# Forgetting attention's value products once a head, with the values stationary on two column halves, and its gate with features on partitions

## The chip, the core and the metric

The kernel runs on one core of a Trainium2 chip. A core has TensorE (the 128x128 array; PE is its matmul queue and PEld its weight loads in the profile), VectorE (DVE), ScalarE (ACT), GpSimd (POOL) and SyncE (SP), which issues most transfers. Each engine works through its own instructions in order and waits on semaphores for the others. The metric is device time in microseconds (us), the median of the runs; lower is better.

## The reference, cut to what matters

Three transformer blocks follow each other on 512 tokens of width 1024. The change touches only the first block, whose input projection is cut into three mixers. The third is forgetting attention, with 8 heads of 64 features:

```python
def _fox_mixer(q, k, v, f_logit, b_f):
    qh, kh, vh = heads(q), heads(k), heads(v)
    log_f = jax.nn.log_sigmoid(f_logit + b_f)
    c = jnp.cumsum(jnp.transpose(log_f, (0, 2, 1)), axis=-1)
    for blk in range(seq // C_BLOCK):          # 4 blocks of 128 queries
        q0, q1 = blk * C_BLOCK, blk * C_BLOCK + C_BLOCK
        s = einsum('bhqd,bhkd->bhqk', qh[:, :, q0:q1], kh[:, :, :q1]) * scale
        s = s + c[:, :, q0:q1, None] - c[:, :, None, :q1]
        p = softmax(where(mask, s, -inf), axis=-1)
        outs.append(einsum('bhqk,bhkd->bhqd', p, vh[:, :, :q1]))
...
y_c = _fox_mixer(c_q, c_k, c_v, c_fl, fox_b_f[layer]) * jax.nn.silu(c_z)
y = jnp.concatenate([y_a, y_b, y_c], axis=-1)
x = x + jnp.einsum('bse,ed->bsd', y, w_out[layer])
```

Query block t looks at the first 128(t+1) keys only, so a head has 1 + 2 + 3 + 4 = 10 pairs of a query tile and a key tile.

## The kernel before, in words

**Dense products.** Every projection is a `Block` of 512 (or 256) columns. The contraction runs over eight chunks of 128 features in four units of two chunks. Activations and weights are each split into a high and a low part (`hH`, `hL`, `wH`, `wL`), and three products replace one. A block of orientation "tok" puts tokens on the output's partitions (activations stationary), one of orientation "feat" puts features there (weights stationary). ACT makes `wH` of the next unit and DVE makes `wL` (`split`), from `wraw`, which SP loads three units ahead.

**The softmax loop.** Attention runs in steps s, one item (head h, query tile t) a step, head by head: items 4h to 4h+3 are head h. Each engine has its own loop, and in step s:

- PE makes the scores of item s in one of two banks (four matmuls, the last two add the decay row and the causal mask), then one side group (six matmuls of a dense block), then transposes the weights of item s-2, then, before the change, the value products of item s-3. The side groups are those of `UV` (512 columns) in steps 0 to 15 and of `AZ` (256 columns) in steps 16 to 35; in steps 1, 5, 9, ..., 29 there is none (`FOX_IDLE`).
- DVE, before the change, first finishes item s-4 (reciprocal of the row sum, then the product with the gate, from PSUM into `merged`), then takes the row maximum of item s, then does extra work of the other two mixers (`gated_mlp`) and splits.
- ACT takes the exponential of item s, copies the transposed weights of item s-2 out of PSUM, then does splits and its part of the extras.
- POOL subtracts for the low part of each head's keys (L602).

**By feature.** Two other attentions of the program, grouped-query (`gqa`) and neighbourhood (`nat`), already work in another form. DVE scales the exponentials of item s-1 by the reciprocal row sum before they are transposed. Once a head, in a step with s % 4 == 2, `head_values` multiplies with the values stationary (64 columns of the array) and the weights moving, the even key tiles on one column half and the odd on the other. In the next step ACT copies one half out of PSUM (L1297) and DVE adds the other (L1955). The result has features on partitions and needs no transposes.

**After the loop.** The block's output product `O0` needs the merged rows with features on partitions. PE transposes chunks 4 to 7 (forgetting attention) and 2 and 3 (the second mixer), ACT and DVE make `hH` and `hL` of each, and `O0` takes its units in the order 4, 6, 2, 0. Chunks 0 and 1 (the gMLP) come in the middle of `O0`.

## Time and profile before

| | before |
|---|---|
| median of 3 runs | 2502.22 us (2500.92 to 2503.83) |
| profiled execution | 2504.66 us, of which the span is 2502.9 us |
| PE busy | 2468.2 us, 99% |
| DVE busy | 1497.7 us, 60% |
| ACT busy | 1111.4 us, 44% |
| POOL busy | 68.8 us, 3% |
| granted TensorE clock, mean | 0.996 |

Times in the trace count from the span's start. The softmax loop of forgetting attention lies at 190.6 to 274.3 us, 3% of the span. PE's busy time includes modelled ends of pipelined matmuls, so the share says little by itself; what counts is how far apart successive instructions start and what an engine waited for.

### The profile page before, as it was taken

To read this page: it belongs to the slowest core of one execution; us is meant where nothing else is said; L and a number is where in the kernel's file an instruction comes from. 1 tells how busy PE (TensorE), PEld (TensorE's weight loads), DVE (VectorE), ACT (ScalarE), POOL (GpSimd) and SP (SyncE) were. 2 spreads that over 40 slices of the span, in tenths; PEclk is the share of its full clock that TensorE was granted. 3 is DMA by queue.
4 is the path that set the end of the run, shared out by engine and by line. 5 is a ranking of instruction groups with operands and counts; after the bars stand their busy time and mean duration, and the time that the engine had idled before them with its cause. 6 is when DMAs were issued, how large, how long until landed. Compare 5 with 4: busy or idle time off the path is not lost.

```text
span 2502.9 us, 31797 instructions
## 1 busy us (share of the span) xinstructions
PE 2468.2 (99%) x12090; PEld 2008.3 (80%) x12090; DVE 1497.7 (60%) x2798; ACT 1111.4 (44%) x1959; POOL 68.8 (3%) x148
## 2 busy tenths in 40 slices
PE   8999999999999999999999999999999999999998
PEld 7888878788777787888888887887787888888887
DVE  6766768653656677544444587645557686544445
ACT  3436455333645656322222344336647572422223
POOL 0001000100000000000000000000000000000000
PEclk9999999999999999999999999999999999999999
DMA  4320223223323231233333242233232212333332
GB/s 151 91 69 22 78 84 124 59 88 93 97 72 94 87 91 51 73 113 101 93 101 93 77 139 66 75 96 110 64 97 80 88 58 89 101 97 97 97 97 88
DMA packets 118967, 221.69 MB, mean 89 GB/s; under 512 B 14352, under 2 KB 21824, under 8 KB 118304
## 3 DMA queue, kind: packets, MB, share of 16 engines
q1 hardware_dynamic: 114192, 201.60, 26.7%
q0 software_dynamic: 4480, 17.79, 2.4%
q8 instruction: 97, 1.59, 0.3%
q14 instruction: 54, 0.44, 0.1%
q10 hardware_dynamic: 144, 0.26, 0.0%
HBM read 215.40 MB, written 4.23 MB: 88 GB/s over the span
## 4 chain that ended last, share of the span: by engine, by line
PE 92%; DVE 4%; ACT 3%; issue 1%; DMA 0%; SPq 0%; ACTq 0%; DVEq 0%
PE bank L686 51%; PE bank L683 28%; PE bank L833 2%; PE bank L910 1%; PE bank L809 1%; PE bank L844 1%; PE bank L810 1%; PE bank L859 1%; PE bank L894 1%; PE bank L948 1%; PE bank L727 0%; DVE tab L1876 0%; ACT sbufPT L1293 0%; ACT sbufS L1279 0%; DMA wraw<-in_w_in_dram 0%
## 5 line engine op out<-in xcount | busy, mean ns | idle before, releaser
L1682 DVE TENSOR_TENSOR wL<-wraw,wH 128x1024 fp32r<-128x1024 f32 (+1 forms) x388 | 460.7, 1187 | 661.0 <-ACT wH L1115 659.1
L1115 ACT ACTIVATE wH<-wraw 128x1024 fp32r<-128x1024 f32 (+1 forms) x388 | 398.5, 1027 | 932.8 <-PE bank L686 576.4
L686 PE MATMUL bank<-hH,wH 128*128 128x512 f32 x1704 | 684.6, 402 | 1.9 <-DVE wL L1682 1.0
L686 PE MATMUL bank<-hL,wH 128*128 128x512 f32 x1704 | 666.0, 391 | 0.0
L686 PE MATMUL bank<-hH,wL 128*128 128x512 f32 x1704 | 665.6, 391 | 0.0
L686 PEld LDWEIGHTS bank<-hH,wH 128*128 128x128 f32 x1704 | 320.6, 188 | 76.0 <-issue 10.5
L686 PEld LDWEIGHTS bank<-hL,wH 128*128 128x128 f32 x1704 | 320.7, 188 | 71.4 <-issue 7.7
L686 PEld LDWEIGHTS bank<-hH,wL 128*128 128x128 f32 x1704 | 320.4, 188 | 68.5
L683 PE MATMUL bank<-wH,hH 128*128 128x512 f32 (+2 forms) x736 | 283.4, 385 | 0.0
L683 PE MATMUL bank<-wL,hH 128*128 128x512 f32 (+2 forms) x736 | 278.3, 378 | 0.0
L683 PE MATMUL bank<-wH,hL 128*128 128x512 f32 (+2 forms) x736 | 278.1, 378 | 0.0
L683 PEld LDWEIGHTS bank<-wH,hH 128*128 128x128 f32 x736 | 139.5, 190 | 26.0 <-DVE wL L1682 0.5
L683 PEld LDWEIGHTS bank<-wL,hH 128*128 128x128 f32 x736 | 139.0, 189 | 25.8
L683 PEld LDWEIGHTS bank<-wH,hL 128*128 128x128 f32 x736 | 139.3, 189 | 24.0
L683 PE MATMUL bank<-wH,yH 128*128 128x512 f32 x352 | 137.2, 390 | 0.0
L683 PE MATMUL bank<-wH,yL 128*128 128x512 f32 x352 | 137.0, 389 | 0.0
L683 PE MATMUL bank<-wL,yH 128*128 128x512 f32 x352 | 136.9, 389 | 0.0
L833 PEld LDWEIGHTS bank<-ident,sbufS 128*128 128x128 f32 x592 | 70.2, 140 | 45.6 <-issue 21.0
L833 PE MATMUL bank<-ident,sbufS 128*128 128x128 f32 x592 | 98.4, 276 | 5.9 <-ACT sbufPT L1293 5.1
L686 PE MATMUL bank<-yH,wH 128*128 128x512 f32 x256 | 100.4, 392 | 0.9 <-ACT yH L1189 0.5
L686 PE MATMUL bank<-yL,wH 128*128 128x512 f32 x256 | 100.0, 391 | 0.2
L686 PE MATMUL bank<-yH,wL 128*128 128x512 f32 x256 | 99.7, 389 | 0.0
(346 smaller groups left out, 3062.8 us busy)
## 6 DMA issues: line engine op xcount, KB each, us to landing
wraw<-in_w_in_dram SPq DMA_DIRECT2D x180, 512.0 KB, 3.6
wraw<-in_w_ffn_down_dram SPq DMA_DIRECT2D x44, 512.0 KB, 3.5
wraw<-in_w_ffn_gate_dram SPq DMA_DIRECT2D x40, 512.0 KB, 3.7
wraw<-in_w_ffn_up_dram SPq DMA_DIRECT2D x40, 512.0 KB, 3.7
wraw<-in_w_out_dram SPq DMA_DIRECT2D x24, 512.0 KB, 3.5
wraw<-in_w_up_a_dram SPq DMA_DIRECT2D x8, 512.0 KB, 3.5
wraw<-in_w_up_b_dram SPq DMA_DIRECT2D x8, 512.0 KB, 3.5
wraw<-in_w_up_c_dram SPq DMA_DIRECT2D x8, 512.0 KB, 3.5
```

The lines of the kernel that those rows point to most:

```text
L683: mm = pe.matmul(bank[t][:, 0:b.cols], act_part[:, k, t * P:(t + 1) * P], w_part[:, kk, :], start=first, stop=last)
L686: mm = pe.matmul(bank[b.bank0 + t][:, :], w_part[:, kk, t * P:(t + 1) * P], act_part[:, k, :], start=first, stop=last)
L809: pe.matmul(dst[:, 0:kmax], q_split[slot][:, tok], k_twice[slot][:, keys], start=True, stop=False)
L810: mm = pe.matmul(dst[:, 0:kmax], q_split[slot][:, tok], k_low[slot][:, keys], start=False, stop=kind != "fox")
L833: mm = pe.transpose(bank[TP][:, c * P:(c + 1) * P], sbufS[:, y % 3, c * P:(c + 1) * P], ident[:, :])
L844: mm = pe.matmul(bank[PV][:, 0:w], sbufPT[:, y % 2, c * P:(c + 1) * P], v[:, c, c0:c0 + w], start=c == 0, stop=c == nk - 1)
L859: mm = pe.matmul(bank[PV][half, :].rearrange("p (t q) -> p t q", t=NT), v[:, c, c0:c0 + w], weights[:, :, c * P:(c + 1) * P], start=c < 2, ...
L894: pe.matmul(bank[SC + pair % 2][:, :], k1[:, h, j * P:(j + 1) * P], q1[:, h, :], start=True, stop=True).then_inc(S["qk_done"], 1)
L910: mm = pe.matmul(dst[:, 0:P + 1], pmat[:, back, sj, t * P:(t + 1) * P], v1a[:, sj, h, :], start=sj == srcs[0], stop=sj == srcs[-1])
L948: mm = pe.matmul(bank[SC + h][:, tok], kl[r, h // 2, tok], ql[r, h // 2, tok], start=True, stop=True)
L1115: A(wH[:, u % W_SLOTS, 0:width], wraw[:, u % RAW_SLOTS, 0:width], ACT.Copy).then_inc(S["w_hi"], 1)
L1682: V.tensor_tensor(wL[:, u % W_SLOTS, 0:width], wraw[:, u % RAW_SLOTS, 0:width], wH[:, u % W_SLOTS, 0:width].bitcast(F32), ALU.subtract).th ...
```

## The change

- `CZ`, the gate's projection, goes from "tok" to "feat", so that the gate lies in `merged` with features on partitions. It has as many matmuls of the same size as before.
- Forgetting attention joins the by-feature form. DVE scales the exponentials before the transposes, `head_values` makes one head's products in four matmuls of 512, 384, 128 and 256 moving columns, ACT copies 384 columns of the other half, and DVE adds the halves and multiplies by the gate. The transposed weights of a head go to `tab` (free by then) instead of `sbufPT`.
- ACT never writes the first 128 tokens of a head's half (key tile 1 isn't seen from query tile 0), so POOL zeroes `ytok[:, :, 0:128]` once.
- The 16 transposes of chunks 4 to 7 fall away. ACT and DVE make `hH` and `hL` of them straight from `merged`, after chunks 2 and 3, and `O0` takes its units in the order 2, 4, 6, 0.
- POOL's load of `final_norm_g` into `ytok` waits for the last head.

```diff
-        "CZ": Block("CZ", w, 0, KD, 3328, 512, "tok"),
-        "O0": Block("O0", o, 0, KD, 0, 512, "tok", order=(4, 6, 2, 0)),
+        "CZ": Block("CZ", w, 0, KD, 3328, 512, "feat"),
+        "O0": Block("O0", o, 0, KD, 0, 512, "tok", order=(2, 4, 6, 0)),
...
 def by_feature(kind):
-    return kind in ("gqa", "nat")
+    return kind in ("fox", "gqa", "nat")
...
+            pool.wait_ge(S["ho_done"], 4)
+            pool.wait_ge(S["low_zero"], 1)
+            pool.memset(ytok[:, :, 0:P], 0.0).then_inc(S["y_zero"], 1)
+            pool.wait_ge(S["y_zero"], 1)
...
-            pool.wait_ge(S["y_ready"], 1)
+            pool.wait_ge(S["y_done"], 32)
             pool.dma_start(yflat[:, 0:D], bcast_rows(a["final_norm_g"], D)).then_inc(S["gp_step"], 16)
...
                 pe.wait_ge(S["ptev"], y + 1)
-                pe.wait_ge(S["y_done"], y + 1 - NT)
-                if kind == "gqa":
+                if y >= NT:
+                    pe.wait_ge(S["y_done"], y + 1 - NT)
+                if kind == "fox":
+                    own, other, _ = feature_rows(it)
+                    for c, half in ((0, own), (1, other), (3, own), (2, other)):
+                        mm = pe.matmul(bank[PV][half, c * P:SEQ].rearrange("p (t q) -> p t q", t=NT - c),
+                                       v[:, c, c0:c0 + w], weights[:, c:NT, c * P:(c + 1) * P], start=c < 2, stop=c >= 2)
+                elif kind == "gqa":
...
-            pe.wait_ge(S["y_done"], n.at("ys"))
-            transposes(merged, (4, 5, 6, 7), None, 0)
             transposes(merged, (2, 3), "y_ready", 1)
+            n("tp", 4)
+            n("tp_hi", 4)
...
                         own, other, g = feature_rows(items[s - 4])
+                        tokens = slice(P if kind == "fox" else 0, SEQ)
                         act.wait_ge(S["pv_done"], nth_y[s - 4] + 1)
-                        A(ytok[own, g, :], bank[PV][other, :], ACT.Copy).then_inc(S["half_moved"], 1)
+                        A(ytok[own, g, tokens], bank[PV][other, tokens], ACT.Copy).then_inc(S["half_moved"], 1)
...
-            hi_chunks((4, 5, 6, 7), hH, lambda k: 0.5)
             hi_chunks((2, 3), hH, lambda k: 0.5)
+            act.wait_ge(S["y_done"], n.at("ys"))
+            for j in range(4):
+                n("tp")
+                A(hH[:, 4 + j, :], merged[:, j, SEQ:D], ACT.Copy, scale=0.5).then_inc(S["tp_hi"], 1)
...
                         then(V.reciprocal(r, total))
-                        if kind == "fox":
-                            dst = merged[:, it["t"], SEQ + it["y"]:SEQ + it["y"] + w]
-                            V.scalar_tensor_tensor(out=dst, in0=src, scalar=r, in1=dst, op0=ALU.mult,
-                                                   op1=ALU.mult).then_inc(S["y_done"], 1)
-                        else:
-                            dst = ytok[:, it["t"], it["y"]:it["y"] + w]
-                            V.tensor_scalar(dst, src, r, None, ALU.mult).then_inc(S["y_done"], 1)
+                        dst = ytok[:, it["t"], it["y"]:it["y"] + w]
+                        V.tensor_scalar(dst, src, r, None, ALU.mult).then_inc(S["y_done"], 1)
...
                         dve.wait_ge(S["half_moved"], n("half_moved"))
-                        V.tensor_tensor(ytok[own, g, :], ytok[own, g, :], bank[PV][own, :], ALU.add).then_inc(
-                            S["y_done"], NT)
+                        if kind == "fox":
+                            if s == 7:
+                                dve.wait_ge(S["y_zero"], 1)
+                            then(V.tensor_tensor(ytok[own, g, :], ytok[own, g, :], bank[PV][own, :], ALU.add))
+                            z = merged[own, g, SEQ:D]
+                            V.tensor_tensor(z, z, ytok[own, g, :], ALU.mult).then_inc(S["y_done"], NT)
+                        else:
+                            V.tensor_tensor(ytok[own, g, :], ytok[own, g, :], bank[PV][own, :], ALU.add).then_inc(
+                                S["y_done"], NT)
...
-            lo_chunks((4, 5, 6, 7), hH, hL, lambda k: 0.5)
             lo_chunks((2, 3), hH, hL, lambda k: 0.5)
+            for j in range(4):
+                n("tp")
+                dve.wait_ge(S["tp_hi"], n("tp_hi"))
+                V.scalar_tensor_tensor(out=hL[:, 4 + j, :], in0=merged[:, j, SEQ:D], scalar=0.5,
+                                       in1=hH[:, 4 + j, :].bitcast(F32), op0=ALU.mult, op1=ALU.subtract).then_inc(
+                    S["tp_free"], 1)
```

Three places show how instructions move; line numbers after the change are a few higher than before. The first is VectorE in steps 19 and 20. L1929 is the row maximum, L1896 and L1899 finish an older item, L1838 to L2232 are extras. Before:

```order
L1896 RECIPROCAL small<-small 128x1
L1899 SCALAR_TENSOR_TENSOR merged<-bank,small,merged 128x64
L1929 TENSOR_REDUCE small<-bank 128x1
L1838 TENSOR_REDUCE small<-set 128x16
L1896 RECIPROCAL small<-small 128x1
L1899 SCALAR_TENSOR_TENSOR merged<-bank,small,merged 128x64
L1929 TENSOR_REDUCE small<-bank 128x1
L2231 TENSOR_SCALAR small<-small 128x16
```

After, where L1939 is the row maximum, L1945 and L1946 scale the exponentials, L1968 adds the halves and L1970 multiplies by the gate:

```order
L1939 TENSOR_REDUCE small<-bank 128x1
L1945 RECIPROCAL small<-small 128x1
L1946 TENSOR_SCALAR sbufS<-sbufS,small 128x384
L1968 TENSOR_TENSOR ytok<-ytok,bank 64x512
L1970 TENSOR_TENSOR merged<-merged,ytok 64x512
L1853 TENSOR_REDUCE small<-set 128x16
L1939 TENSOR_REDUCE small<-bank 128x1
L1945 RECIPROCAL small<-small 128x1
L1946 TENSOR_SCALAR sbufS<-sbufS,small 128x512
L2248 TENSOR_SCALAR small<-small 128x16
```

The finishing product of 64 columns, which stood ahead of the maximum, is replaced by a scaling as wide as the item behind it, and in the step with s % 4 == 3 the sum and the gate's product stand between the scaling and the next maximum, behind a wait for ACT's copy.

The second place is PE in step 14, from the side group's last matmuls to the next item's scores. Before:

```order
L683 MATMUL bank<-wH,hH 128x512
L683 MATMUL bank<-wH,hL 128x512
L683 MATMUL bank<-wL,hH 128x512
L833 MATMUL bank<-ident,sbufS 128x128
L844 MATMUL bank<-set,sbufPT 128x64 x4
L809 MATMUL bank<-yL 128x512
```

After:

```order
L687 MATMUL bank<-wH,hH 128x512
L687 MATMUL bank<-wH,hL 128x512
L687 MATMUL bank<-wL,hH 128x512
L864 MATMUL bank<-tab,set 64x512
L864 MATMUL bank<-tab,set 64x384
L864 MATMUL bank<-tab,set 64x128
L864 MATMUL bank<-tab,set 64x256
L837 MATMUL bank<-ident,sbufS 128x128
L813 MATMUL bank<-yL 128x512
```

The value products of every step (L844, here those of one item) become four matmuls a head ahead of the transpose, in every fourth step.

The third place is PE at the end of the loop, from the last side group to the first matmuls of `O0`, as the difference; 24 transposes become 8.

```order
-L683 MATMUL bank<-wH,hH 128x256
-L683 MATMUL bank<-wH,hL 128x256
-L683 MATMUL bank<-wL,hH 128x256
-L727 MATMUL bank<-ident,merged 128x128 x24
-L683 MATMUL bank<-wH,hH 128x512
+L687 MATMUL bank<-wH,hH 128x256
+L687 MATMUL bank<-wH,hL 128x256
+L687 MATMUL bank<-wL,hH 128x256
+L731 MATMUL bank<-ident,merged 128x128 x8
+L687 MATMUL bank<-wH,hH 128x512
```

## Rows read from the trace of the kernel before

**Rows 1.** The page: busy time of each engine.

```profile
PE 2468.2 (99%) x12090; PEld 2008.3 (80%) x12090; DVE 1497.7 (60%) x2798; ACT 1111.4 (44%) x1959; POOL 68.8 (3%) x148
```

**Rows 2.** Stretches: head 2, the later heads by DVE's steps, two units of `O0`.

```profile
core 0: us, PE busy (x) PEld busy (x) DVE busy (x) ACT busy (x) POOL busy (x), PEclk, DMA share, GB/s
...
211.35:221.15 9.80, 9.80 (x67) 8.38 (x66) 4.68 (x14) 5.93 (x15) 1.78 (x1) 1.00 0.11 28
...
221.86:268.00 46.14, 43.80 (x322) 38.07 (x320) 39.56 (x95) 35.46 (x88) 6.19 (x4) 1.00 0.13 41
...
277.38:282.90 5.52, 5.52 (x27) 4.56 (x26) 3.12 (x5) 1.86 (x3) 0.00 (x0) 1.00 0.23 72
```

**Rows 3.** Who DVE waited for, 221.86 to 268.00 (us, times, longest).

```profile
DVE set L2202 <- ACT set L1395: 1.6, 1, 1.6
DVE small L1896 <- PE bank L844: 1.1, 3, 0.7
DVE set L2214 <- ACT set L1410: 1.0, 2, 0.5
DVE small L1929 <- PE bank L815: 0.8, 3, 0.4
DVE wL L1682 <- ACT wH L1115: 0.5, 1, 0.5
DVE yL L1852 <- ACT yL L1228: 0.2, 1, 0.2
```

**Rows 4.** PE in order of time, steps 22 and 23: start, length, what.

```profile
247.36 0.97 PEld L844 LDWEIGHTS bank<-set,sbufPT 128*128 128x128 f32 x8
...
248.28 0.48 PE L809 MATMUL bank<-yL 128*128 128x512 f32 x1
...
249.12 0.37 PE L683 MATMUL bank<-wH,hH 128*128 128x256 f32 x1
```

**Rows 5.** The same view, grouped-query attention: one head's values.

```profile
649.06 1.94 PE L859 MATMUL bank<-tab,set 128*64 128x512 f32 x8
```

**Rows 6.** DVE in order of time, steps 19 and 20.

```profile
240.83 0.68 DVE L1929 TENSOR_REDUCE small<-bank 128x1 f32<-128x512 f32 x1
...
242.68 0.16 DVE L1896 RECIPROCAL small<-small 128x1 f32<-128x1 f32 x1
242.87 0.28 DVE L1899 SCALAR_TENSOR_TENSOR merged<-bank,small,merged 128x64 f32<-128x64 f32 x1
243.07 0.28 DVE L1929 TENSOR_REDUCE small<-bank 128x1 f32<-128x128 f32 x1
```

**Rows 7.** Lines of DVE: scaling (two widths), sum, product of two tensors (ns min/median/max).

```profile
L1936 DVE TENSOR_SCALAR sbufS<-sbufS,small x32: 485/487/491, 626.5 to 713.1; 128x512 f32<-128x512 f32 x32
...
L1936 DVE TENSOR_SCALAR sbufS<-sbufS,small x32: 352/354/355, 781.9 to 851.8; 128x256 f32<-128x256 f32 x32
...
L1955 DVE TENSOR_TENSOR ytok<-ytok,bank x32: 678/686/693, 643.9 to 1939.7; 64x512 f32<-64x512 f32 x32
...
L1719 DVE TENSOR_TENSOR x<-x,ytok x4: 691/692/692, 305.3 to 309.3; 128x512 f32<-128x512 f32 x4
```

**Rows 8.** ACT in order of time behind the maximum at 240.83.

```profile
241.55 0.69 ACT L1281 ACTIVATE sbufS<-bank,small 128x512 f32<-128x512 f32 x1 [2.11 <-DVE small L1929]
...
242.23 0.38 ACT L1293 ACTIVATE sbufPT<-bank 128x256 f32<-128x256 f32 x1
```

**Rows 9.** Waits in grouped-query (first) and neighbourhood attention (second).

```profile
DVE ytok L1955 <- ACT ytok L1297: 10.1, 6, 1.8
...
PEld bank L833 <- DVE sbufS L1936: 4.0, 8, 0.9
```

**Rows 10.** The end of the loop and start of `O0`, in order of time.

```profile
268.00 0.15 DVE L1896 RECIPROCAL small<-small 128x1 f32<-128x1 f32 x1
...
274.86 0.42 DVE L1821 SCALAR_TENSOR_TENSOR merged<-set,bank 128x256 f32<-128x256 f32 x1 [0.26 <-ACT set L1155]
...
277.41 0.49 PE L683 MATMUL bank<-wH,hH 128*128 128x512 f32 x1
```

More of the change, by code:

```diff
@@ L458, in head_weights @@
         def head_weights(kind):
-            return view(tflat, 0, (NT, SEQ)) if kind == "gqa" else view(ptflat, 0, (NT, NAT_KEYS))
+            return view(ptflat, 0, (NT, NAT_KEYS)) if kind == "nat" else view(tflat, 0, (NT, SEQ))
         gained = view(gflat, 0, (NT, SEQ))
@@ L480, in build @@
             vn_ready mix_done lam_dot lam_exp out_done a_ready y_squared low_zero
-            scan_out scan_rows m_done p_scaled half_moved
+            scan_out scan_rows m_done p_scaled half_moved y_zero
         """.split()
@@ L1286, in softmax @@
                         if by_feature(kind):
-                            act.wait_ge(S["pv_done"], y - it["t"])
-                            turned = head_weights(kind)[:, it["t"], :]
+                            if y >= NT:
+                                act.wait_ge(S["pv_done"], y - it["t"])
+                            turned = head_weights(kind)[:, it["t"], 0:it["kmax"]]
                         else:
```

## The prediction

> **What bounds the kernel now.** The page's busy times come first [rows 1]: PE is busy 99% of the span, DVE 60%. That suggests that any PE time saved is time won. But the change lies in 84 us, so I read the stretches there next [rows 2]. In head 2 (head 1 reads the same) PE is busy all 9.80 us and DVE 4.68: PE bounds. From DVE's step 12 (its maximum of item 12, at 221.86) to its step 32 (268.00) it is another picture: of 46.14 us DVE is busy 39.56. Third, DVE's waits there [rows 3]: they add up to 5.2 us, 1.9 on PE and 3.3 on ACT. The remaining 1.4 us are gaps between instructions. So DVE has 5.2 us to spare in 46, and that is what the reader should carry into the change, which gives PE less work and DVE more.
>
> **PE's side of the change.** A step's four value products are eight records, whose weight loads start 0.11 us apart ((0.97 - 0.19) / 7) [rows 4]. Ten pairs a head are 20 records, 2.2 us. Afterwards a head has four matmuls of 512, 384, 128 and 256 columns, 1280 in all. Grouped-query attention has four of 512 in 1.94 us, also on two halves [rows 5]; by columns that is 1.2 us, and I take 1.25. A saving of 1.0 us a head, 8 in all, if PE is what everything waits for. `CZ` keeps its number and size of matmuls, so nothing there.
>
> The Trainium skill (TensorEngine Tiling (Array Packing), Stationary-Streaming Swap in Performance Considerations) recommends just this swap where the moving side is 64 wide or less. By the row a head costs 1.25 us; if the halves did not overlap it would be about 2.1, and PE's saving would be gone.
>
> **DVE's side, head by head.** Removed: four finishing products, which start 0.20 us ahead of what follows [rows 6] though they last 0.28; 0.8 us. The reciprocals stay (0.19 to what follows). Added:
> - Four scalings. 512 columns take 0.487 and 256 take 0.354 [rows 7]; by the slope 384 take 0.42 and 128 take 0.29. Less the same 0.08 of overlap each: 1.22 us.
> - The sum of the halves, 0.69, and as its successor waits for it, 0.72 [rows 7].
> - The gate's product, two tensors of 512 columns: 0.69 by the nearest row [rows 7], 0.61 with overlap. Its bounds are 0.4 (two scalings' rate) and 0.7.
>
> That is 1.22 + 0.72 + 0.61 - 0.8 = 1.75 us more a head. Steps 12 to 31 hold five such heads: 8.7 us.
>
> **The new wait.** In the step with s % 4 == 3 DVE takes the maximum of item s, scales item s-1, and then waits for ACT's copy of the other half. ACT, in order, first has to take the exponential of item s (which needs that very maximum), then copy the transposes of s-2. From the row at 240.83: ACT begins at +0.72, its copy of 256 columns at +1.40 [rows 6, 8], the half's copy 0.31 later and takes 0.49 (an estimate from 0.38 for 256 columns), so DVE's sum starts at +2.25. DVE is through with its scaling at 0.60 + 0.19 + 0.42 = 1.21. It stands still for 1.04 us, however far PE is ahead, and nothing of its own lies between. Five heads: 5.2 us. Grouped-query attention shows the same wait: 10.1 us in 6 times [rows 9], 1.7 each, with PE's part in it. Behind the waiting sum stand on DVE the gate's product, the extras, the weight split and the next maximum; ACT's next exponential and PE's transposes two steps on wait for these.
>
> **The middle, summed.** DVE's work is 39.56 + 1.4 + 8.7 = 49.7 us, already over the 46.14 it had. With 5.2 of the new wait it is 54.9; I let all 5.2 of the old waits vanish, since DVE now arrives late everywhere. PE has 43.80 - 5 = 39 us of work there, so DVE bounds and PE stands. The middle grows by 8.7 us. Bounds: the gate's product at 0.4 takes 1.0 off; ACT's part of the old waits staying adds 3.3.
>
> **Before it.** By step 12 PE has saved 21 pairs (4.7 us) less two heads of 1.25: 2.2 us. But DVE is late once. After PE's step 7 ends, ACT still needs 0.2 + 0.31 + 0.49 and DVE 0.72 + 0.61 = 2.3 us till the next maximum, and in that step a weight split of 1.2 stands in between. The scaling of item 7 (0.20 + 0.19 + 0.49 later) is then ready at +4.4. PE gets to its transpose after 2.6 us: scores, about 0.4 and 0.5 (0.84 for 512 columns, [rows 4]), six side matmuls of 0.23 (24 in 5.52 us, [rows 2]), three transposes of 0.11. It waits 1.8. So PE's step 12 begins 0.4 earlier, at 220.7, but DVE's maximum in it comes 2.3 behind that instead of 0.7: at 223.0 or so, 1.2 late.
>
> **Behind it.** From DVE's step 32 to the first matmul of `O0` it was 9.4 us [rows 10]. Afterwards DVE has: a scaling with reciprocal 0.6, two extras of 1.2, a split of 1.2, four gates of the gMLP at 0.36, the sum and product 1.3, then two low chunks 1.3: 8.3 us, without a gap that I see. 1.0 us is won. The 16 dropped transposes don't count for more: ACT and DVE make chunks 2 and 3 while PE has nothing else. The four other chunks (0.62 on ACT and 0.68 on DVE each) lie under the first unit of `O0`, 5.5 us. POOL's memset waits for the second mixer's last output, before step 0, and what stands behind it in POOL's queue, the low keys of head 2, is asked for in step 4 at the earliest. Its load of the gain moves from step 31 behind the last head and is used after `O0`, some 22 us later; both cost nothing. Without that cover the load would add its few us once. SP's queue has the same transfers in the same order, but for the units of `O0`.
>
> **Sum.** 8.7 + 1.2 - 1.0 = 8.9 us. The profiled execution, 2504.66, becomes 2513.6; it stands 2.4 above the median, so the median of 2502.2 becomes 2511.
>
> **A page's rule on the product.** A head's gate product costs 0.61 us by a row of equal form. The Trainium skill (VectorE: DVE Perf Modes, Mode 2x_2P) says that a float32 tensor_scalar out of SBUF runs twice as fast as a float32 tensor_tensor. The trace agrees: 256 more columns cost the scaling 0.133 us [rows 7], and 512 of two tensors 0.69. By the other rate the sum would be 1.6 us less over eight heads.
>
> **The rivals.**
> - *Forecast: DVE bounds from step 12 on, and its wait for ACT is new.* 0.5. 2508 to 2514.
> - *The wait is covered.* DVE's extra work counts, but the half's copy is there in time. Neighbourhood attention speaks for it, where PE waited for the scaling only 4.0 us in 8 times [rows 9]; against it, there table work lies in the gap and here nothing does. 8.9 - 5.2 gives 2506; with the cheaper product 2505. 0.2.
> - *PE bounds throughout; the other side.* DVE follows PE all the way. Then 8 x 1.0 and 1.0 at the end are won: 2493 to 2495. It decides if DVE's additions a head stay under its spare 1.0 us (5.2 / 5) in the middle; they are 1.75 without any wait. 0.06. Something between this and no change, 0.06.
> - *The old waits stay or more come.* ACT's extras and splits go on being late (3.3 us), or the halves don't overlap (0.9 a head in heads 1 and 2), or PE's idle time brings its clock down, which is 1.00 through the loop [rows 2]: 2514 to 2519. 0.18.
> - The Trainium skill (TensorEngine Tiling, PSUM Bottleneck) warns that tiling speeds TensorE but not the emptying of PSUM, which may become the limit. Here it would be the forecast's way, since the half's copy and sum are that emptying.
>
> **How the numbers follow.** About 0.2%, 5 us, is what a measurement of this kernel can tell from none. The forecast and the last rival lie over +5 us: 0.68, of which I move 0.02 to no change for times at 2507. Within it: the covered wait (0.2), that 0.02 and half of the middle case (0.03), 0.25. Faster: 0.09, the other side and the rest. The range takes the covered wait in below from 2504 and most of the added waits above, to 2517; about 0.1 is left out on either side.
>
> **What would show it.** In the trace of the changed kernel: DVE's stretch from its maximum of item 12 to the reciprocal of item 31 should be near 55 us, with waits of about 1 us in front of the sum (L1968) on ACT's copy in all late heads; PE should wait for the scaling (L1946) before transposes (L837), some 8 to 12 us in all. The four value products should take 1.2 to 1.3 us. `O0` should start near 286. I am wrong if DVE shows idle time on PE of more than 3 us in that stretch, or if the sum waits for nothing.

## The result, and the profile after

| | before | after |
|---|---|---|
| median | 2502.34 us (2500.92 to 2503.83, 4 runs) | 2522.93 us (2521.97 to 2528.45, 4 runs) |
| profiled execution / its span | 2504.66 / 2502.9 | 2521.97 / 2520.2 |
| PE busy | [rows 1] | 2460.5 us, 98% |
| DVE busy | [rows 1] | 1512.3 us, 60% |
| granted clock, mean | 0.996 | 0.995 |

The ratio is 1.0085 (95% interval 1.0071 to 1.0100): slower by 20.6 us. The forecast was 2511 (2504 to 2517). The direction was right, the size less than half of what came.

The page after, busy times (line numbers after the change: scores L813 to L819, transposes L837, value products L864, maximum L1939, scaling L1946, sum L1968, gate product L1970, ACT's copy of the transposes L1304 and of the half L1309):

```profile
PE 2460.5 (98%) x11978; PEld 1995.4 (79%) x11978; DVE 1512.3 (60%) x2814; ACT 1115.4 (44%) x1967; POOL 68.0 (3%) x149
```

PE lost 7.7 us of work and DVE gained 14.6, and the median rose by 20.6 (the two profiled executions differ by 17.3). PE, which was busy 99% of the span, has less to do than before, so what was lost is waiting. The stretches that answer to [rows 2] (length, then busy times of PE, PEld, DVE, ACT, POOL, the granted clock, the DMA share, GB/s):

```profile
220.53:285.04 64.51, 43.64 (x260) 34.26 (x258) 50.31 (x105) 39.62 (x94) 5.32 (x4) 0.89 0.10 29
285.04:294.01 8.97, 5.95 (x32) 4.69 (x32) 8.17 (x15) 4.82 (x11) 0.56 (x1) 0.81 0.23 66
```

From the maximum of item 12 to the reciprocal of item 31 it was 46.14 us and is 64.51, 18.4 more where 8.7 were forecast. The way to `O0` takes 8.97. The mean clock of that stretch is 0.89; it was 1.00. DVE's waits in it, and those of PE's weight loads (us in total, times, longest):

```profile
DVE ytok L1968 <- ACT ytok L1309: 6.9, 5, 2.5
DVE small L1939 <- PE bank L819: 4.4, 4, 2.7
DVE set L2219 <- ACT set L1407: 1.0, 1, 1.0
...
PEld bank L837 <- DVE sbufS L1946: 17.2, 6, 4.0
```

DVE waits 12.3 us, not 5.2: for the half as foretold, but also 4.4 us for scores. An engine that is the bound doesn't wait for the one behind it. And PE stands 17.2 us for the scaling, up to 4.0 at a time. One head in order of time (start, length, what, idle time before and its releaser) shows both:

```profile
242.04 0.68 DVE L1939 TENSOR_REDUCE small<-bank 128x1 f32<-128x512 f32 x1
...
244.34 0.69 DVE L1968 TENSOR_TENSOR ytok<-ytok,bank 64x512 f32<-64x512 f32 x1 [1.10 <-ACT ytok L1309]
245.14 0.69 DVE L1970 TENSOR_TENSOR merged<-merged,ytok 64x512 f32<-64x512 f32 x1
245.86 1.22 DVE L1853 TENSOR_REDUCE small<-set 128x16 f32<-128x1024 f32 x1
247.11 0.29 DVE L1939 TENSOR_REDUCE small<-bank 128x1 f32<-128x128 f32 x1
...
247.51 0.49 DVE L1946 TENSOR_SCALAR sbufS<-sbufS,small 128x512 f32<-128x512 f32 x1
247.79 0.48 ACT L1304 ACTIVATE tab<-bank 128x384 f32<-128x384 f32 x1
248.42 1.08 PE L837 MATMUL bank<-ident,sbufS 128*128 128x128 f32 x4 [3.52 <-ACT tab L1304]
...
254.28 0.69 DVE L1939 TENSOR_REDUCE small<-bank 128x1 f32<-128x512 f32 x1 [0.87 <-PE bank L819]
```

A head falls into two parts, and these carry all that follows. The **near part** runs from the maximum of the head's widest item (item 19, 512 columns, at 242.04) to that of the next head's first (item 20, 247.11). The **far part** runs from there to the next widest item (254.28). In the near part DVE has, one behind the other, the wait for the half, the sum, the product and an extra of 1.22 us, and only then the maximum of item 20 and the scaling of item 19, for which PE stands since 244.9. The same two parts of four heads each, first of the kernel before (items 15 to 28), then of the changed one; the first row is one near part, the second row the sum of the four near ones, the third that of the far ones:

```profile
240.83:243.07 2.24, 1.92 (x15) 1.74 (x15) 2.17 (x5) 1.05 (x3) 0.00 (x0) 1.00 0.64 202
...
sum 9.19, PE 8.45 PEld 7.71 DVE 8.91 ACT 6.08 POOL 0.03; mean PE 2.11 PEld 1.93 DVE 2.23 ACT 1.52 POOL 0.01
...
sum 26.91, PE 25.39 PEld 21.93 DVE 21.83 ACT 21.33 POOL 4.89; mean PE 6.35 PEld 5.48 DVE 5.46 ACT 5.33 POOL 1.22
```

```profile
242.04:247.11 5.07, 1.64 (x13) 1.27 (x12) 3.77 (x7) 1.53 (x4) 0.00 (x0) 1.00 0.36 107
...
sum 21.76, PE 9.92 PEld 8.49 DVE 15.20 ACT 9.54 POOL 0.00; mean PE 2.48 PEld 2.12 DVE 3.80 ACT 2.38 POOL 0.00
...
sum 30.22, PE 24.62 PEld 18.94 DVE 24.10 ACT 20.43 POOL 4.03; mean PE 6.16 PEld 4.73 DVE 6.03 ACT 5.11 POOL 1.01
```

Before, DVE was busy 97% of the near parts and PE 94% of the far ones. Of DVE's 5.4 us of idle time here 5.1 lay in the far parts. The change adds 6.3 us of DVE's work and 5.8 us of waits for the half to the near parts, which grow from 9.19 to 21.76. The far parts grow from 26.91 to 30.22, though PE has less to do there.

### The profile page after: what moved, and what is told of

It reads as the page before. It is cut to its first block, busy times and chain, and to the rows that moved or that the text cites. A ratio compares the mean times of both kernels' runs of the same rounds, so it can differ in the third digit from the quotient of the medians.

```text
span 2520.2 us, 31577 instructions
## 1 busy us (share of the span) xinstructions
PE 2460.5 (98%) x11978; PEld 1995.4 (79%) x11978; DVE 1512.3 (60%) x2814; ACT 1115.4 (44%) x1967; POOL 68.0 (3%) x149
## 4 chain that ended last, share of the span: by engine, by line
PE 90%; DVE 5%; ACT 3%; issue 2%; DMA 0%; SPq 0%; ACTq 0%; DVEq 0%
PE bank L690 51%; PE bank L687 26%; PE bank L837 2%; PE bank L920 1%; PE bank L813 1%; PE bank L814 1%; PE bank L869 1%; PE bank L904 1%; PE bank L848 1%; PE bank L958 1%; DVE hL L1800 1%; DVE tab L1891 0%; PE bank L731 0%; DVE sbufS L1936 0%; DMA wraw<-in_w_in_dram 0%
## 5 line engine op out<-in xcount | busy, mean ns | idle before, releaser
L690 PE MATMUL bank<-hH,wH 128*128 128x512 f32 x1736 | 696.9, 401 | 1.6 <-ACT hH L1199 0.9
L690 PE MATMUL bank<-hL,wH 128*128 128x512 f32 x1736 | 678.1, 391 | 0.0
L690 PE MATMUL bank<-hH,wL 128*128 128x512 f32 x1736 | 677.5, 390 | 0.0
L690 PEld LDWEIGHTS bank<-hH,wH 128*128 128x128 f32 x1736 | 326.4, 188 | 77.7 <-issue 11.1
L690 PEld LDWEIGHTS bank<-hL,wH 128*128 128x128 f32 x1736 | 326.3, 188 | 72.4 <-issue 7.7
L690 PEld LDWEIGHTS bank<-hH,wL 128*128 128x128 f32 x1736 | 326.2, 188 | 69.8
L687 PE MATMUL bank<-wH,hH 128*128 128x512 f32 (+2 forms) x704 | 270.8, 385 | 2.3 <-DVE hL L1800 2.3
L687 PE MATMUL bank<-wH,hL 128*128 128x512 f32 (+2 forms) x704 | 265.7, 377 | 0.0
L687 PE MATMUL bank<-wL,hH 128*128 128x512 f32 (+2 forms) x704 | 265.7, 377 | 0.0
L687 PEld LDWEIGHTS bank<-wH,hH 128*128 128x128 f32 x704 | 133.9, 190 | 26.9 <-DVE hL L1800 2.5
L837 PE MATMUL bank<-ident,sbufS 128*128 128x128 f32 x592 | 100.9, 281 | 27.8 <-ACT tab L1304 21.1
L837 PEld LDWEIGHTS bank<-ident,sbufS 128*128 128x128 f32 x592 | 71.2, 142 | 70.0 <-DVE sbufS L1946 30.1
```

What stands on the lines that cost most here:

```text
L687: mm = pe.matmul(bank[t][:, 0:b.cols], act_part[:, k, t * P:(t + 1) * P], w_part[:, kk, :], start=first, stop=last)
L690: mm = pe.matmul(bank[b.bank0 + t][:, :], w_part[:, kk, t * P:(t + 1) * P], act_part[:, k, :], start=first, stop=last)
L837: mm = pe.transpose(bank[TP][:, c * P:(c + 1) * P], sbufS[:, y % 3, c * P:(c + 1) * P], ident[:, :])
```

## The experiments

I kept four theories. A: DVE's load sets the pace. B: the halved clock behind PE's waits is part of the loss. D, later sharpened to E: what counts is where DVE's work stands, ahead of what PE waits for. F: ACT's copies, in order behind exponentials that wait for DVE, carry its lateness on. "Near" and "far" in this table are the four parts of items 15 to 31 together in the profiled execution, in us, worked out from the starts of DVE's maxima. Each ratio is to the kernel before in the same rounds, whose median was 2501.5 to 2502.4 us. Where the intervals of two rows overlap, their medians alone don't tell them apart.

| kernel | median us | ratio to before (95%) | near | far |
|---|---|---|---|---|
| before | 2502.3 | | 9.19 | 26.91 |
| after | 2522.9 | 1.0085 (1.0071 to 1.0100) | 21.76 | 30.22 |
| after, again | 2524.7 | 1.0092 (1.0077 to 1.0107) | 21.77 | 30.32 |
| fillers, first try | 2538.3 | 1.0141 (1.0126 to 1.0156) | 21.83 | 40.32 |
| fillers in the value bank, from step 17 | 2521.7 | 1.0076 (1.0061 to 1.0091) | 21.80 | 26.46 |
| the same, from step 9 | 2521.6 | 1.0082 (1.0067 to 1.0097) | 21.78 | 26.97 |
| load alone, near | 2514.0 | 1.0045 (1.0030 to 1.0060) | 14.94 | 30.62 |
| load alone, far | 2506.6 | 1.0020 (1.0010 to 1.0029) | 9.34 | 29.86 |
| scaling alone | 2506.4 | 1.0016 (1.0006 to 1.0025) | 10.24 | 28.47 |
| sum and product later | 2512.3 | 1.0040 (1.0025 to 1.0055) | 9.84 | 33.01 |
| the same, copy first | 2508.8 | 1.0028 (1.0018 to 1.0038) | 9.83 | 30.64 |
| one half | 2510.8 | 1.0034 (1.0022 to 1.0046) | 12.74 | 29.60 |
| one half, extras later | 2509.2 | 1.0031 (1.0020 to 1.0042) | 8.40 | 33.70 |
| the same, copy first | 2506.1 | 1.0014 (1.0005 to 1.0024) | 8.29 | 30.70 |
| one half, all later | 2514.1 | 1.0051 (1.0036 to 1.0066) | 6.45 | 40.23 |
| the same, copy first | 2508.6 | 1.0020 (1.0010 to 1.0030) | 6.12 | 34.19 |
| after without scaling | 2528.2 | 1.0102 (1.0085 to 1.0119) | 22.16 | 32.63 |
| the same, copy first | 2521.1 | 1.0074 (1.0057 to 1.0091) | 22.11 | 28.85 |
| after, copy first | 2523.0 | 1.0083 (1.0068 to 1.0098) | 21.86 | 29.10 |
| before, copy first | 2502.0 | 0.9997 (0.9988 to 1.0006) | 9.59 | 26.45 |

**Sum and product one step later** (the changed kernel):

```
-  if by_feature(kind) and s >= 7 and s % NT == 3:
-      own, _, g = feature_rows(items[s - 4])
+  late = int(kind == "fox")
+  if by_feature(kind) and s >= 7 + late and s % NT == (3 + late) % NT:
+      own, _, g = feature_rows(items[s - 4 - late])
```

> The changed kernel, with one edit: DVE's sum of the two halves and the gate's product stand one step later for forgetting attention, behind the next maximum and the next scaling, so that ACT's copy of the other half has been there for long. Theory A (DVE's work and its wait for ACT's half copy are what sets the loop's pace): the five waits of 1.1 to 2.5 us in front of the sum (6.9 us in steps 12 to 31) go, PE's wait for the next scaling gets shorter by about as much, and the time falls by 5 to 8 us, to 2515 to 2518. Theory B (the larger part of the loss is PE's halved clock after its long waits): the waits for the scaling fall under 3 us, the clock stays at 1.00 through the loop, and the time falls by more than the waits removed: 10 us or more, under 2513. Rival C (ACT's own work or PE is what the loop waits for, and DVE's wait only fills slack): no change, 2521 to 2525.

2512.3, 10.6 less, with the same work. That is more than the waits removed (6.9). The trace still shows the clock at half from 246 to 250 us and a DVE wait of 2.71 for PE behind it. Which theory owns the surplus this run doesn't tell; the fillers below put the clock at some 3 us, which would cover it but doesn't prove it.

**All value products on the head's own half** (four matmuls into `bank[PV][own]`, no half copy, no sum):

> The changed kernel with the value products of forgetting attention all on the head's own column half: no copy of the other half by ACT, no sum by DVE, and no zeroing by POOL; DVE multiplies the gate with the bank directly. A head costs PE about 0.9 us more, DVE 0.7 less, ACT 0.4 less, and the wait of about 1.1 us is gone. Theory A: 1.8 us a head less on DVE over six heads is 11 less, and 1 to 2 more where PE bounds in the first heads: 2511 to 2514. Theory B: as PE's waits get shorter the clock stays up as well: 2505 to 2509. Rival C (the emptying of the bank is no bound, PE's matmul time counts): 2524 to 2530.

2510.8, just under A's range and above B's, at a clock of 1.00 from item 12 to the end of the loop.

**The scaling alone, in the kernel before** (`by_feature` scaling and PE's wait for it in fox too; the finishing product no longer scales):

> The kernel before with one edit: DVE scales the exponentials of forgetting attention by the reciprocal ahead of the transposes, as in the changed kernel, and the value products stay per item as before, with a finishing product that no longer scales. This adds 1.22 us a head to DVE (four scalings less overlap) and puts DVE between the exponential and PE's transposes; PE's work is that of before. Theory A: DVE has 5.2 us to spare in steps 12 to 31 and gets 6.1 more: 2503 to 2506. Theory B: PE's dependence on the scaling brings waits of several us and a lower clock by itself: 2508 to 2516. Rival C: the scaling costs nothing: 2501 to 2503.

2506.4: 4.0 more, just above A's range and well below B's. DVE's eight times 1.22 us are paid to two fifths. So putting DVE between the exponential and the transposes costs little by itself.

**Fillers, first try** (ten matmuls of 512 columns behind ACT's last copy, before the wait for the scaling):

> The changed kernel with ten matmuls more of 512 columns (their result is never read) on PE in steps 17, 21, 25, 29 and 33 of forgetting attention, between the scores and the transposes that wait for the scaling: they fill about 2.2 us of the 4 us that PE stands there. They are put there to keep its clock from falling. Theory B (the four stretches at half clock, 17 us together, make PE late for DVE): the granted clock stays at 1.00 up to the end of the loop, and the time falls by 4 to 8 us, to 2515 to 2519. Theory A alone (DVE paces the loop, PE at half clock has time enough): the clock stays up and the time is the same within 1 us, 2522 to 2524. If the fillers end later than the scaling, the time rises by up to 5 us.

2538.3, outside all that was expected. The fillers' row shows why:

```profile
256.88 4.64 PE L831 MATMUL bank<-hH 128*128 128x512 f32 x10 [3.44 <-ACT tab L1308]
```

PE had already stood 3.44 us for the copy. The clock had fallen, each filler took 0.46 us, and they ended behind the scaling. It only shows what late work on PE costs there.

**Fillers in the bank of the value products:**

```
   elif by_feature(kind):
+      if kind == "fox" and s in (17, 21, 25, 29, 33):
+          pe.wait_ge(S["y_done"], nth_y[s - 2] + 1 - NT)
+          for _ in range(8):
+              pe.matmul(bank[PV][:, :], hH[:, 0, 0:P], hH[:, 1, :], start=True, stop=True)
       pe.wait_ge(S["p_scaled"], n("p_scaled"))
```

> The filler once more, where it can start early. In the run with ten fillers PE first stood 3.4 us until ACT had copied the transposes before, the clock fell, and the fillers ran at half of it and ended after the scaling, so that run said nothing on the clock. Here eight matmuls of 512 columns go into the bank of the value products, which is free once DVE has made the last head's gate product, about 1 us after PE's scores; 1.7 us at full clock, in steps 17, 21, 25, 29 and 33. Theory B (the halved clock behind the waits is what makes the loop longer than the forecast): PE's waits without work are under 2 us, the granted clock is 1.00 up to the last head, and the time falls by 3 to 7 us against the changed kernel, to 2516 to 2520. Theory A alone (DVE's work and its wait are all of the loss): the clock stays up and the time is 2522 to 2524.

2521.7. The clock is 1.00 from 218 us to the end of the loop, and the time barely moves: it misses B's 2516 to 2520 and lies beside A's 2522 to 2524.

**The same in steps 9 and 13 too, beside the changed kernel again:**

> The changed kernel once more, unchanged, so that the fillers and the other edits have it beside them on the same chip. All theories: 2522 to 2524, with a spread of some us from the heads in which the clock happens to fall.

> The fillers of the bank of the value products (eight matmuls of 512 columns) in steps 9 and 13 too, so that no head from the second on is left with a wait of 3 us and more; in the run before the clock had fallen at 212 to 218 us, ahead of the first filler, and stayed at 1.00 behind it. Theory B (part of the loss is the halved clock): the clock is 1.00 from 196 us to the end of the loop, and the time is 3 to 5 us under that of the changed kernel in the same rounds. Theory A alone: within 1 us of it.

2521.6 against 2524.7 in the same rounds, 3.1 less; the intervals overlap. (The changed kernel itself came 0.7 above the 2522 to 2524 expected.) The profiled stretches say it more sharply. The far parts with fillers:

```profile
235.73:244.15 8.42, 6.32 (x44) 4.72 (x43) 7.23 (x19) 6.18 (x15) 1.28 (x1) 1.00 0.00 0
249.23:255.87 6.64, 6.64 (x34) 4.98 (x33) 5.50 (x12) 5.86 (x14) 1.39 (x1) 0.78 0.00 0
260.19:266.39 6.20, 5.98 (x38) 4.40 (x37) 5.99 (x14) 5.37 (x13) 1.38 (x1) 1.00 0.27 89
273.35:279.06 5.71, 4.89 (x33) 3.35 (x32) 5.38 (x13) 2.85 (x9) 0.00 (x0) 1.00 0.28 92
sum 26.97, PE 23.83 PEld 17.45 DVE 24.10 ACT 20.25 POOL 4.05; mean PE 5.96 PEld 4.36 DVE 6.03 ACT 5.06 POOL 1.01
```

The clock was still at half for a moment in the second, so the expectation of 1.00 throughout did not hold. But the sum is 26.97, that of before, and the near parts keep their 21.78. So B is right for some 3 us: the growth of the far parts is the halved clock. In these four heads the whole rest of the loss stands in the near parts, 3.15 us a head. In the changed kernel the near parts of heads 1 and 2 grew too, from 2.30 to 5.11 and from 2.24 to 4.02.

**Load without dependency, near and far** (the kernel before, two unread products a head; the first in s % 4 == 3, the second in s % 4 == 1):

```
+  if kind == "fox" and s >= 7 and s % NT == 3:
+      g = 2 + (s // NT) % 2
+      then(V.tensor_tensor(ytok[0:DH, g, :], q2[0:DH, 0, :], q2[0:DH, 1, :], ALU.mult))
+      then(V.tensor_tensor(ytok[0:DH, g, :], q2[0:DH, 0, :], q2[0:DH, 1, :], ALU.mult))
   if extra:
```

> The kernel before, with DVE's load alone: in each step with s % 4 == 3 from 7 on DVE makes two tensor products more of 64 by 512 (two of 0.7 us, 1.4 a head; their result is never read), where the changed kernel has its sum and gate product. Nothing waits for them but what stands behind them on DVE. Theory A: 1.4 by five heads is 7 us in a stretch where DVE had 5.2 us of waits: these go first, so +2 to +4 us at the loop's end: 2504 to 2506. Theory D (load without a dependency is hidden; the loss comes from the path): 2502 to 2503.

> The kernel before with the same eight pairs of unread tensor products (1.4 us a head) as in the run with the load alone, but in the steps with s % 4 == 1 instead of 3, ahead of the extras. In s % 4 == 3 they cost 11.9 us, 8 x 1.4 = 11.2. Theory A (any us of DVE's counts when DVE has used up its waits): again 8 to 12 us, 2510 to 2514. Theory E (only what stands between the maximum of a head's widest item and the maximum of the next head's first item is on the chain through DVE, ACT and PE; elsewhere PE's work lies beside it): 2 to 6 us, 2504 to 2508.

11.9 us near and 5.1 far, for the same eight pairs. That is the cleanest evidence for E. The eight places don't match at the ends: two near pairs (steps 31 and 35) stand behind the last maximum and one far pair (step 33), and from item 3 to item 15 neither place costs more than 0.3 us. But in the four heads of items 15 to 31, where both kernels have four pairs, it is 9.5 us against 3.1. Near, the near parts grow by 5.75 (the load's full length), and the far parts by 3.7, with the clock at half for 3.4 us in three of the four. Far, the heads' far parts grow by 0.82, nothing, 0.76 and 1.37:

```profile
242.68:250.57 7.89, 7.42 (x43) 6.50 (x44) 4.52 (x13) 6.08 (x14) 1.29 (x1) 0.78 0.01 2
```

```profile
240.56:246.98 6.42, 6.15 (x46) 5.17 (x45) 6.15 (x15) 5.86 (x14) 1.28 (x1) 1.00 0.04 14
```

The first row is the far part behind a loaded near part: the clock is 0.78 and it takes 7.89. The second holds the load itself, DVE 6.15 instead of 5.27, and takes the 6.42 of before.

**The scaling left out of the changed kernel** (DVE's `tensor_scalar` skipped, PE waits for the exponential):

> The changed kernel without the scaling of the exponentials: DVE still takes the reciprocals, but forgetting attention's weights are not divided by their sum (that part of the computation is left out), and PE's transposes wait for ACT's exponential alone. The wait for ACT's half copy, the sum and the gate's product stay. This takes 1.22 us a head off DVE and takes DVE out of the path from the exponential to the transposes. Theory A (DVE's load counts, each us of it): 5 to 6 heads of 1.22 are 6 to 7 us less, 2515 to 2517. Theory D (the scaling's place in the path, behind DVE's sum, product and extras, is what makes PE stand, and its clock fall): PE's waits of 3 to 4 us go, the clock stays at 1.00, and the time falls by 12 us or more, under 2511.

2528.2, the wrong way for both. PE stood at the same place as long, for another releaser:

```profile
PEld bank L839 <- ACT sbufS L1293: 16.4, 5, 4.1
...
PE bank L839 <- ACT tab L1306: 15.8, 5, 4.0
```

In the head shown above, ACT's copy of item 18 (247.79) stands behind the exponential of item 20, which waits for the same maximum. This began F. (The expectations below call these items 14 and 16; by the count in the trace they are 18 and 20.)

**Extras later, all later** (one-half kernel; first the extra of s % 4 == 3 goes behind the widest item's scaling, then the product too):

> The kernel with all value products on one half, with one edit more: in the steps with s % 4 == 3 DVE's extra work (a grouped sum or a product of up to 1.22 us) stands behind the next maximum and the scaling of the head's widest item instead of ahead of them. DVE's work is the same. Theory A (DVE's load alone): no change against that kernel, 2509 to 2512. Theory D (what stands ahead of the scaling that PE waits for is what costs): PE's waits for the scaling get up to 1.2 us shorter in four heads, DVE's waits for the next scores (4.5 us) get shorter behind them, 2505 to 2508.

> The kernel with the values on one half, where DVE's gate product stands one step later and the extras of s % 4 == 3 behind the scaling of the widest item: between the maximum of the widest item and the maximum of the next head's first item DVE has one scaling and at most a weight split. DVE's work is that of the one-half kernel (45.9 us in steps 12 to 31 and 1.5 of gaps). Theory E: DVE's other waits shrink to 1 or 2 us, and the time is 2 to 5 us under the run with the extras alone moved (2509.2): 2504 to 2507. Theory A (load alone): 2508 to 2510. Rival: ACT's exponential of the next item is not what PE waits for, and the later product only delays the bank: over 2510.

2509.2 is A's number, not D's: DVE still waited 4.3 us for scores. The near parts fell by 4.3 us against the one-half kernel and the far parts took 4.1 of them back. And at 2514.1 E's last claim fell: with the near parts down to 6.45 us the far ones took 40.23. The rival named there was nearer. PE's value products need ACT's copy of the widest item, which stands behind the exponential of the item two later and so behind DVE's maximum of s % 4 == 1, now late:

```profile
PEld bank L862 <- ACT tab L1303: 7.5, 4, 2.3
...
DVE small L1938 <- PE bank L817: 6.8, 4, 3.8
```

**Copy first** (ACT, steps with s % 4 of 0 and 1 of fox, in four kernels):

```
-  exponential of item s; copy of item s-2
+  first, second = (take_copy, take_exp) if kind == "fox" and s % NT in (0, 1) else (take_exp, take_copy)
+  first()
+  second()
```

> The changed kernel with ACT's order turned in the steps with s % 4 of 0 and 1 of forgetting attention: ACT copies the transposes of item s-2 out of their bank first and takes the exponential of item s behind that (elsewhere, as before, the exponential comes first). In the changed kernel the copy of item 14 begins at 247.79, behind the exponential of item 16, which waits for DVE's maximum at the end of its sum, product and extras, while its transposes were in the bank at 244.5; the copy of the widest item, which the value products need, stands likewise behind the next maximum. Theory F (these copies carry DVE's lateness on to PE): PE's waits for copies shrink, but its wait for the scaling at the same place (17.2 us) stays, so 1 to 4 us less, 2519 to 2522. Theory E alone (only DVE's own order counts): 2522 to 2524.

> The same turned order of ACT's copy and exponential on the kernel with one half and the extras of s % 4 == 3 behind the scaling (2509.2). There PE's value products wait for ACT's copy of the widest item (6.1 us in steps 12 to 31). Theory F: these waits go, DVE's 4.3 us of waits for scores go for the larger part, 2505 to 2508. Theory E alone: 2508 to 2510. Rival: the exponential that now stands behind the copy comes late, and the time rises: over 2511.

> The turned order on the kernel with the gate product later too (2514.1, where I had expected 2504 to 2507). In its trace the value products waited 8.4 us for ACT's copy of the widest item, which stood behind the exponential and so behind DVE's maximum of item s with s % 4 == 1, and DVE in turn waited 11.0 us for scores that stand behind the value products on PE. Theory F: with the copy ahead of the exponential these 8.4 us go and most of the 11.0: 2504 to 2508. If the later product is bad for another reason (the bank, DVE's work itself): 2512 to 2515.

> The turned order of ACT's copy and exponential in the kernel before. There PE waits 1.4 us in twice for these copies in steps 12 to 31, and DVE 1.9 for PE. Theory F: at most these go: 2499 to 2502. Rival: an exponential behind a copy that waits for late transposes: 2503 to 2506.

In the all-later kernel 5.4 us went, half a microsecond short of F's range, and items 15 to 31 show the two waits nearly gone:

```profile
PEld bank L862 <- ACT tab L1307: 1.7, 2, 1.4
...
DVE small L1945 <- PE bank L817: 0.7, 1, 0.7
```

That is clear of the noise. The one-half kernel with extras later came 3.1 lower, in F's range, but the intervals overlap. The changed kernel lost nothing that can be told (2523.0: E's range, not F's), nor did the kernel before. F holds, as far as these four show, where DVE's scaling isn't late at the same place.

**Two links at once:**

> The kernel with both halves and with sum and product one step later (2512.3), with ACT's copy ahead of its exponential in steps with s % 4 of 0 and 1. In its trace the value products waited 7.7 us for ACT's copy of the widest item. Theory F: with DVE's scaling no longer behind the sum, the copy is the last link, and 3 to 6 us go: 2506 to 2509. If the two halves with their sum are what costs: 2511 to 2513.

> The kernel without the scaling of the exponentials (forgetting attention's weights are again not divided by their sum; that part is left out), which was slower than with it (2528.2), with ACT's copy ahead of its exponential in steps with s % 4 of 0 and 1. In the trace without the scaling PE stood 3.6 us at 251.37 for ACT's copy of item 14, 250.75 to 251.24, which stood behind the exponential of item 16 and so behind DVE's half copy wait, sum, product and extras. Theory F: with scaling and copy both out of the way PE no longer stands there, 2.5 us in six heads: 2510 to 2516. If the copy's order isn't why that run was slow: 2524 to 2530.

2508.8, 3.5 less, in F's range, though the intervals overlap. Without scaling 2521.1: 7.1 less (the intervals just overlap), but far above the 2510 to 2516 expected. PE now stood at a third link, the next scores, whose bank the exponential of item s % 4 == 0 frees:

```profile
PEld bank L813 <- ACT sbufS L1295: 9.2, 4, 2.5
```

So the scaling, the copy and that exponential wait side by side for one and the same block of DVE. Taking away one or two leaves the third; of what was tried, only a shorter block helps by much (sum later: near parts 9.84). That the kernel without scaling is slower than with it I can place (far parts 32.63 at a clock of 0.60 to 0.76), but why its clock fell for longer was not tried.

No version beats the kernel before. The best of the changed form, 2506.1, has 38.99 us in these eight parts with DVE busy 36.73; before they were 36.10. So DVE's busy time alone is now longer than all eight parts were before, by 0.6 us, and the other 2.3 of the 2.9 are its waits and gaps.

## Why the prediction was wrong, by its own steps

- **Right: the direction and the new wait.** The sum waited 1.10 us in four of the five late heads (1.04 forecast). In the other it was 2.48, behind two table loads of 1.28 us on ACT that also stood in the kernel before. Sum and product took 0.80 and 0.72 to what follows (0.72 and 0.61).
- **Right: PE's saving.** A head's values took 1.30 us at full clock (1.25), 2.40 at half.
- **Wrong: "I let all 5.2 of the old waits vanish, since DVE now arrives late everywhere", and "DVE bounds and PE stands".** This is the step that failed. It treated 46 us as one balance, DVE's spare time against DVE's new work. The two lie in different parts of a head. The sum, the gate's product and their wait are in the near part, where DVE was busy 97%, and all of them lengthen the head. The spare time was in the far part, of which PE filled 94%, and that part doesn't get shorter: 26.91 us before, 26.97 after at nearly full clock (30.22 without the fillers). What holds it there after the change, with PE and DVE each busy under 90% of it (23.83 and 24.10 us), stays open. The waits in the stretch were 12.3 us instead of 5.2: 6.9 for the half, 1.0 for ACT, 4.4 for PE. PE waited 17.2 us for the scaling where I had said 8 to 12. My own mark for being wrong, over 3 us of idle time on PE, was met.
- **Half seen: the clock.** It was in the fourth rival as one of several ways, without a place. Behind PE's stands of 3.6 to 4.0 us it was at half in the loop, and DVE waited for the slow scores, about 3 us in all. With that clock nearly restored the loss is still 20 us, so it isn't the main cause.
- **Mis-sized: DVE's work.** 50.31 us busy in the stretch against 48.3. All of that is time beside POOL (last section): a scaling of 256 columns took 1.23 us instead of 0.35, and the four remainders of key splits 5.78 us together instead of 4.43.
- **Before and behind.** Item 12 came at 220.53, not 223.0, since in this execution PE came to its first scores 3.2 us sooner, out of a shorter stretch at half clock ahead of the loop (3.4 us against 10.2). That is luck, and in this execution it hides 3.2 us of the loss. From there to item 12 it was 30.1 us against 28.2: 1.9 more where 1.2 were forecast. The tail took 8.97 (8.3; a gap of 0.59 for the half stands in it), a gain of 0.4 and not 1.0.
- **The sum.** 9.6 us more in the middle than forecast, made of 7.1 waits, 2.0 work and 0.5 gaps. The profiled execution misses the forecast 2513.6 by 8.4; the median misses by 11.9, as this execution lay 1.0 below its median and that of before 2.3 above.
- **The Trainium skill** (TensorEngine Tiling (Array Packing), PSUM Bottleneck) warned that the emptying of PSUM may become the limit. The runs agree in part: without half copy and sum it is 12.1 us less, but moving the same sum and product to a later step already wins 10.6 us, so here their place counts for more than their amount.

## What to carry to other kernels

Cut the loop's period at the points where one engine hands over to the other, and make the balance in each part, not over the loop. Spare time in one part doesn't pay for work in another: the same 1.4 us a head cost 11.9 us in one place and 5.1 in the other, in the four late heads 9.5 and 3.1. Look for everything that waits behind the block that you make longer, in each engine's own order; where three things wait for it side by side, taking one away did nothing here or made it worse, and moving the block won half of the loss.

## What the runs showed of the hardware that was not expected

**The clock falls inside a busy loop.** Before, the clock was 1.00 from 196 us to the end of the loop. In the changed kernel it fell to 0.50 (1.2 GHz) at the end of PE's stands of 3.96, 3.63 and 4.02 us. The length of one stand doesn't settle it: a stand of 2.85 us that ended at 259.86 brought no fall, and in the run with the load near the clock fell to 0.50 from 231.6 to 235.0 us, behind a stand of 1.8. One such stretch, and the values at either level:

```profile
272.19:279.02 6.83, 5.96 (x24) 4.32 (x24) 4.99 (x10) 2.56 (x8) 0.00 (x0) 0.50 0.25 79
```

```profile
251.85 1.30 PE L864 MATMUL bank<-tab,set 128*64 128x512 f32 x8
...
273.03 0.72 PEld L837 LDWEIGHTS bank<-ident,sbufS 128*128 128x128 f32 x4 [4.02 <-DVE sbufS L1946]
...
276.56 2.40 PE L864 MATMUL bank<-tab,set 128*64 128x512 f32 x8
```

**POOL and DVE block each other.** The remainder of a key split is made by DVE for one half and by POOL for the other:

```profile
202.58 0.69 DVE L1867 SCALAR_TENSOR_TENSOR yH<-set,yH 64x512 fp32r<-64x512 f32 x1 [0.22 <-ACT yH L1238]
202.69 1.73 POOL L606 TENSOR_TENSOR yH<-set,yH 64x512 fp32r<-64x512 f32 x1 [14.56 <-ACT yH L1238]
...
238.90 1.28 POOL L606 TENSOR_TENSOR yL<-set,yL 64x512 fp32r<-64x512 f32 x1 [12.27 <-ACT yL L1238]
238.97 1.76 DVE L1867 SCALAR_TENSOR_TENSOR yL<-set,yL 64x512 fp32r<-64x512 f32 x1
```

Whichever starts first runs at its own speed or close to it (DVE 0.69; POOL 1.28, in two later heads 1.38 and 1.37), and the other is held up: POOL 1.73 instead of 1.28, DVE 1.76 instead of 0.69. When DVE comes late it is DVE that pays, 1 us. The Trainium skill (SBUF — State Buffer, Terms) says that the two share a port pair that is held for a whole instruction; the trace agrees.
